# An eighth place for experts' weights in the second layer, another order of ring units in the first, and GpSimd's small loads behind the first two blocks

## The reference, cut to what matters

```
for l in range(2):
    mod = silu(cond) @ mod_w[l] + mod_b[l]            # 1024 x 6144 weights per layer
    sh1, sc1, g1, sh2, sc2, g2 = split(mod, 6)
    h = rms(x, norm_g[l, 0]) * (1 + sc1) + sh1
    if l == 0: out = ab_mixer(h, ab_in_w, ..., ab_out_w)   # HGRN2 recurrence | attention
    else:      out = hyena(h, hy_in_w, ..., hy_out_w)      # long convolution
    x = x + g1 * out
    h = rms(x, norm_g[l, 1]) * (1 + sc2) + sh2
    x = x + g2 * moe(h, router_w, router_b, w_gate[l], w_up[l], w_down[l])

def moe(h, ...):                                      # 16 experts, top 2 of one group of 4
    gates = routing weights, tokens x 16
    a = einsum('td,edf->etf', h, w_gate)              # w_gate, w_up: 16 x 1024 x 512
    b = einsum('td,edf->etf', h, w_up)
    hid = silu(a) * b * gates
    return einsum('etf,efd->td', hid, w_down)         # w_down: 16 x 512 x 1024
```

## Time and profile before

| | before |
|---|---|
| median of three runs | 874.86 us (872.3 to 875.55) |
| profiled execution | 872.13 us |
| its span | 869.9 us |
| TensorE busy | 820.4 us, 94% of the span |
| HBM read | 290.10 MB, 335 GB/s over the span |
| mean granted TensorE clock | 0.988 |

### The profile page before, as it was taken

How to read it: one execution, slowest core, us unless ns; L and a number is a source line. 1 busy time by engine, 2 the same in 40 slices (tenths; PEclk the granted TensorE clock), 3 DMA queues, 4 the chain that set the end, 5 groups by cost and what they waited for, 6 DMA issues and landing times.

```text
span 869.9 us, 13266 instructions
## 1 busy us (share of the span) xinstructions
PE 820.4 (94%) x5760; PEld 514.4 (59%) x5760; DVE 284.2 (33%) x587; ACT 176.4 (20%) x308; POOL 37.9 (4%) x67
## 2 busy tenths in 40 slices
PE   4999999799899999999999999999899999999997
PEld 3867778687643555345536888788643555345434
DVE  2155533614631211112114844662531212121113
ACT  4056013411511110111013212300411101110111
POOL 5000000030300000000000000000210000000000
PEclk8999999999999999999999999999899999999999
DMA  9999866652999999999999869255599999999981
GB/s 307 387 312 369 303 225 239 245 193 97 406 418 405 422 429 429 428 429 428 429 407 386 296 245 333 100 192 196 209 387 394 419 430 429 428 429 429 428 364 50
DMA packets 60004, 292.53 MB, mean 336 GB/s; under 512 B 2993, under 2 KB 5158, under 8 KB 47604
## 3 DMA queue, kind: packets, MB, share of 16 engines
q1 hardware_dynamic: 57940, 289.69, 83.5%
q10 hardware_dynamic: 1248, 1.08, 0.5%
q0 software_dynamic: 768, 1.04, 0.5%
HBM read 290.10 MB, written 1.70 MB: 335 GB/s over the span
## 4 chain that ended last, share of the span: by engine, by line
PE 70%; DMA 20%; DVE 7%; issue 1%; ACT 1%; SPq 1%; DVEq 0%
PE ps L1887 20%; DMA ring<-in_moe_w_up 17%; PE ps L1910 7%; PE ps L2018 6%; PE ps L1477 4%; PE ps L1541 4%; PE ps L1873 4%; PE ps L1663 3%; PE ps L1749 3%; PE ps L1535 3%; PE ps L1516 3%; PE ps L1923 2%; DMA ring<-in_mod_w 2%; PE ps L2014 1%; DVE hs L1117 1%
## 5 line engine op out<-in xcount | busy, mean ns | idle before, releaser
L1887 PE MATMUL ps<-ring,arena 128*64 128x512 f32 x896 | 224.7, 593 | 12.4 <-DMA ring<-in_moe_w_up 10.7
L1887 PEld LDWEIGHTS ps<-ring,arena 128*64 128x64 f32 x896 | 75.8, 137 | 118.6 <-issue 116.6
L1910 PE MATMUL ps<-ring,arena 128*64 128x512 f32 x512 | 113.4, 595 | 1.1 <-ACT arena L798 1.1
L1910 PEld LDWEIGHTS ps<-ring,arena 128*64 128x64 f32 x512 | 36.2, 137 | 66.4 <-issue 63.2
L1268 DVE SCALAR_TENSOR_TENSOR arena<-ps,arena 128x256 f32<-128x256 f32 x32 | 20.0, 668 | 163.0 <-PE ps L1887 163.0
L2018 PE MATMUL ps<-hs,ring 128*128 128x256 f32 x320 | 70.3, 380 | 0.0
L2018 PEld LDWEIGHTS ps<-hs,ring 128*128 128x128 f32 x320 | 60.5, 190 | 9.3 <-issue 1.4
L1873 PE MATMUL ps<-arena 128*128 (+1 forms) x512 | 60.0, 275 | 0.0
L1873 PEld LDWEIGHTS ps<-arena 128*128 128x128 f32 x512 | 58.4, 192 | 0.4 <-issue 0.4
L1887 PE MATMUL ps<-hs,arena 128*64 128x512 f32 x128 | 56.3, 593 | 0.0
L1477 PE MATMUL ps<-ring,csil 128*32 128x128 f32 x1536 | 51.2, 290 | 4.4 <-DVE arena L909 4.1
(11 more groups left out here) (310 smaller groups left out, 837.5 us busy)
## 6 DMA issues: line engine op xcount, KB each, us to landing
ring<-in_moe_w_up SPq DMA_DIRECT2D x32, 2048.0 KB, 17.2
ring<-in_moe_w_down SPq DMA_DIRECT2D x32, 2048.0 KB, 13.3
ring<-in_mod_w SPq DMA_DIRECT2D x24, 2048.0 KB, 12.7
ring<-in_moe_w_gate SPq DMA_DIRECT2D x24, 2048.0 KB, 13.9
hs<-in_moe_w_gate SPq DMA_DIRECT2D x8, 2048.0 KB, 17.4
ring<-in_hy_in_w SPq DMA_DIRECT2D x6, 2048.0 KB, 12.7
ring<-in_ab_in_w SPq DMA_DIRECT2D x4, 2048.0 KB, 13.1
ring<-in_ab_in_w SPq DMA_DIRECT2D x5, 1024.0 KB, 18.7
```

Of the source, the lines that this page charges most:

```text
L1887: ins = mm(bank(4 + w)[e * 64:e * 64 + 64, :], xg[:, k, e * 64:e * 64 + 64], weights[:, k, :], start=(k == 0), stop=(k == KD - 1))
L1910: ins = mm(bank(6 + half)[e * 64:e * 64 + 64, :], hidT[:, f, e * 64:e * 64 + 64], down_unit(n + 4 + e)[:, f, half * 512:half * 512 + 512], ...
```

## The change

Three edits. First, in layer 1 a second extra place, `late_spare`, for the gate of the pair's second expert in even pairs (odd pairs have it in its ring place), with an own order of the loads. Second, modulation blocks 14 and 15 come ahead of the two units of the output projection in the ring's order, so they have places 1 and 2, and the output projection places 3 and 4; the four small tables are now loaded behind both units of the output projection. Third, GpSimd waits for the arrival of modulation blocks 0 and 2 before its eleven small loads.

```
+UNITS += MODS[14:16]
 OUT0_AT = len(UNITS)
-UNITS += [("about", 0), ("about", 1)] + MODS[14:16]
-
+UNITS += [("about", 0), ("about", 1)]
...
+        late_spare = arena[:, 11776:11776 + UNIT].rearrange("p (k c) -> p k c", k=KD)
...
-                    if n == OUT0_AT + 3:
+                    if n == OUT0_AT + 2:
...
-                def load_gate(i, dst):
-                    sp.wait_ge(ring_free[n % RING], i + (n // RING - 1))
-                    arrived(sp, n, i - 1)
-                    load(i, 0, dst)
+                def load_gate(i, j, dst):
+                    m = n + j
+                    sp.wait_ge(ring_free[m % RING], i + (m // RING - 1))
+                    arrived(sp, m, i - 1)
+                    load(i, j, dst)
+                if l == 0:
...
+                else:
+                    sp.wait_ge(q["t_y"], 2)
+                    arrived(sp, n + 1 - RING)
+                    load(0, 1, late_spare)
+                    load_in_place(0, (0,))
+                    load_gate(1, 1, unit(n + 1))
+                    load_in_place(0, (2, 3, 4, 5))
+                    sp.wait_ge(q["t_htm"], 2 * l + 2)
+                    load_gate(1, 0, spare)
+                    for i in range(1, NPAIR):
+                        if i > 4:
+                            load_in_place(i, (2, 3, 4, 5))
+                        if i == 4:
+                            load_in_place(i, (2, 3))
+                        if i + 1 < NPAIR:
+                            load_gate(i + 1, 0, unit(n) if i % 2 else spare)
+                            load_gate(i + 1, 1, late_spare if i % 2 else unit(n + 1))
+                        if i == 4:
+                            load_in_place(i, (4, 5))
+                        if i < 4:
+                            load_in_place(i, (2, 3, 4, 5))
...
+            for m in (0, 2):
+                arrived(pool, MOD_AT[m])
...
-                                weights = spare if odd and w == 0 and e == 0 else unit(n + 2 * w + e)
+                                weights = unit(n + 2 * w + e)
+                                if w == 0 and e == 0 and odd:
+                                    weights = spare
+                                elif w == 0 and e == 1 and l == 1 and not odd:
+                                    weights = late_spare
```

More of the change, by code:

```diff
@@ L481, in load_in_place @@
                         load(i, j, down_unit(m) if j >= 4 else unit(m))
-                def load_gate(i, dst):
-                    sp.wait_ge(ring_free[n % RING], i + (n // RING - 1))
-                    arrived(sp, n, i - 1)
-                    load(i, 0, dst)
[L489 to L496, removed]
+                def load_gate(i, j, dst):
[4 more added lines that the diff above has]
+                if l == 0:
+                    load_in_place(0, range(6))
+                    sp.wait_ge(q["t_htm"], 2 * l + 2)
+                    load_gate(1, 0, spare)
+                    for i in range(1, NPAIR):
+                        load_in_place(i, (1,))
+                        if i + 1 < NPAIR:
[8 more added lines that the diff above has]
+                    load_in_place(0, (2, 3, 4, 5))
+                    sp.wait_ge(q["t_htm"], 2 * l + 2)
+                    load_gate(1, 0, spare)
+                    for i in range(1, NPAIR):
+                        if i > 4:
+                            load_in_place(i, (2, 3, 4, 5))
+                        if i == 4:
+                            load_in_place(i, (2, 3))
+                        if i + 1 < NPAIR:
+                            load_gate(i + 1, 0, unit(n) if i % 2 else spare)
+                            load_gate(i + 1, 1, late_spare if i % 2 else unit(n + 1))
+                        if i == 4:
+                            load_in_place(i, (4, 5))
+                        if i < 4:
+                            load_in_place(i, (2, 3, 4, 5))
                 n += 6 * NPAIR
```

## The result

The changed kernel took 866.18 us (median of six runs, 865.59 to 869.36), the kernel before 873.24 us (six runs, 871.88 to 875.55). The ratio is 0.9943 with a 95% interval of 0.9921 to 0.9965: faster, by 0.35 to 0.79%. (The two medians by themselves lie 7.1 us apart, which is 0.9919. The text goes by the ratio.) The profiled execution took 866.14 us, with a span of 863.9 us where it was 869.9.

The account below looks back on a forecast made before the run. Bound by DMA in the experts, with TensorE close behind: 29.4 against 27.49 us a pair. Layer 1 -4.1, layer 0 +0.3, start -0.3 us: 874.86 - 4.1 = 870.8 us; range 868.7 to 872.2, 8 in 10 within 867.3 to 873.6.

Parts of the forecast that it names:

- dry issue: Expert loads: a unit issued into a nearly empty queue lands 8.4 to 9.9 us later, taken as 9.3.
- pair 3's wait: Layer 1: TensorE's wait of 0.77 us at pair 3's ups stays.
- The downs of pair 4: Layer 1: landing at 765.9, wanted at 766.25, close but in time.
- The detail of 0.2 us: Layer 1, pair 2's first gate: the other gate now stands behind it on SP, costing 0 to 0.5 us.
- a loss of 0.3 us: Layer 0's other ring order: two-unit lead lost at a dry queue; bounds 1.0 us gain, 0.8 loss.
- The small loads: Start: GpSimd's eleven loads cost 1.2 us of DMA; moving them removes block 2's 0.28 us wait, gain 0.3.
- B: Rival: nothing lost at dry issues, layer 0 gains 1.0; 7.1 us gained in all, 867.8 us; chance 0.20.
- C: Rival: layer 1's lead does not arrive, pair 4's downs hold TensorE; 1.6 us gain, 873.3 us; chance 0.17.
- D: Rival: queue runs dry at every pair's downs from pair 5 on; slower, 878.1 us; chance 0.06.
- E: Rival: shifted times bring or spare a half-clock stretch of TensorE; 1.7 us either way, 869.1 or 872.5; chance 0.09.
- The estimate of 6.8 us: Expert loads: the skill's rule, 2.0 us fixed plus bytes at 436 GB/s, gives 2 MiB issue to landing.

Follow-up runs that it names:

- The place without the turn: Kernel before plus layer 1's eighth place; all pairs keep the order next gates, then ups, then downs: 0.9991.
- the turn without the place: Kernel before, seven places; in layer 1 from pair 4 on a pair's ups go ahead of gate 0 of the next pair: 0.9967.
- place and turn alone: Changed kernel without its two other edits: layer 1's eighth place, and ups ahead of next gates from pair 4; 0.9919 to the kernel before.
- the three with the turn in layer 0: Changed kernel with ups ahead of the next pair's gate 0 from pair 4 in layer 0 too, first run: 0.9895, 861.64 us; two further runs follow.
- ring order as before: Changed kernel with that order in layer 0 too, but blocks 14 and 15 put back behind the output projection: 0.9885, 861.89 us.
- again: Changed kernel with that order in layer 0 too, run once more on the same chip as the one with ring order put back: 0.9902, 862.15 us.

## Why the prediction was right, and where it was off

**The mechanism.** The rows of before gave two paces, 27.49 us for TensorE and 29.4 for DMA, and the statement that the place brings nothing until the order turns at pair 4. The place without the turn and the turn without the place show both halves of it. The waits went at pairs 4 to 6 and a small one came at pair 7's ups, as forecast. The reading of the page was off by one or two slices, and no term uses it: counted from one, the rate stands at 428 to 430 GB/s in slices 15 to 20 and 33 to 38.

**Layer 1, mis-sized.** Forecast 4.1 us, measured 5.62 in the pair of profiles. Over all profiles layer 1 takes 224.7 to 225.5 us with neither place nor turn (five, mean 225.2) and 219.4 to 220.7 with both (five, mean 220.0): 5.1 us, at the upper bound of 5.1 that went with 8.4 us for each dry issue. The term that was mis-sized is the 9.3 us for a dry issue. The ups of pair 4 took 9.6 us from issue to landing, the downs of pair 5 8.3. The first of these downs landed at 780.7 and not at 782.6: 1.0 us is the shorter landing, 0.9 the earlier issue (772.45 instead of 773.3), and so pair 7's ups waited 0.39 us, not 1.4. The issue was earlier because pair 3's wait, forecast to stay, was gone: the downs of pair 1, a dry issue too, landed after 8.7 us instead of 9.7. That is scatter: with place and turn this wait is 0, 0.99, 0.67, 0 and 0.51 us in five profiles (the order is changed kernel, place and turn alone, then the three with the turn in layer 0: first, ring order as before, again), and layer 1 takes 219.5, 220.7, 220.2, 219.4 and 220.3 us, longer where this wait is. With the wait at 0.99 the gain was 4.4 us, close to the 4.1 that were forecast with it in place. The downs of pair 4, close by the working, landed at 765.2 and did not wait.

Two smaller terms were off. The detail of 0.2 us shows as pair 1's ups landing 0.8 us later, counted from the first gate product (32.4 instead of 31.6), for which nobody waited. And the last down products were to start 10.6 us after pair 7's ups, with their weights there at 846.2; they started 11.0 us after them, since they waited 0.73 us for a unit that landed at 845.5. The last two units took 11.0 us to land (834.55 to 845.53) and not 9.8. The kernel before had the same (837.46 to 848.53), where TensorE came too late to notice.

**Layer 0, not contradicted.** Forecast a loss of 0.3 us, measured 0.55 in the two profiles and nothing that can be told in the run times (1.0006). That 0.3 and 0.55 are close is luck: in the seven profiles that have layer 0's order of before, its experts take 224.0 to 227.4 us (mean 225.4), and the two with the new ring order alone 224.8 and 224.9. What the forecast had right is that no wait shrinks. Counted from the first gate product, gate 1 of pair 1 landed after 15.5 us where it was 17.0 before, since its issue took 8.3 us and not 9.9. But the first down of pair 1 took 9.5 us where it was 8.4, and landed after 38.0 us where it was 37.0. So in this pair the lead lived one step longer than the working had it, and was gone at the next.

**The start, right in size as far as the profiles tell, with a term too small.** The small loads delay block 2 by 3.2 us in the mean of the profiles and not by 1.2. The working took the rate of one window of 5 us (295 against 387 GB/s), while the loads were in flight from 7.6 to about 20 us. What was forecast as the gain, 0.28 us, is the wait of that one profile; others without the edit waited from nothing up to 1.22 us for block 2 and 0.85 us for the next unit. In the changed kernel's 0.79 us, 0.43 are the earlier arrival of `x_sample` (7.82 instead of 8.25), which lies anywhere from 7.6 to 9.1 in these profiles. So what the edit brings in a single run lies between nothing and 2 us, the mean of 0.3 us at the projection's start agrees with the forecast, and the run times do not settle it.

**The sum.** -4.1 us was forecast, and the ratio of 0.9943 is -5.0 on 873.24 (-3.1 to -6.9 by its interval). In the pair of profiles it was -6.0, and there the missing part lies mainly in layer 1, 1.5 us, and at the start, 0.5 us. The absolute 866.18 us lies 1.1 below the stated range; the kernel before, too, ran 1.6 us below the 874.86 that the forecast started from once it had six runs. Of the rivals, B (nothing lost at dry issues, and layer 0 gains) has a number for layer 1, 5.8 us, that the 5.62 of this pair comes close to, but not for its reason: pair 4's ups still landed 7.1 us after the unit ahead of them and pair 5's downs 5.7 us, where 4.89 would be no loss. Its second half, a gain in layer 0, did not come. C and D did not come: pair 6's ups landed at 805.2, after pair 5's downs had been used at 799.97. E did not show in this pair of profiles: the same half-clock stretches appear in both, from about 15 to 22 us and at about 141, 158 and 616 us. In other profiles stretches are missing, with a price that can be read off (last section).

The estimate of 6.8 us for a 2 MiB load, which the prediction worked out from the Trainium skill's fit for loads that GpSimd issues ("DMA: Bandwidth & Descriptors", section "Anatomy of one DMA — SWDGE (gpsimd) path"), was not seen. These loads are SyncE's: the lowest of any 2 MiB load in these profiles is 7.6 us, and 8.0 among the expert loads.

## What to carry to other kernels

When TensorE and DMA are within a few per cent, follow the landings unit by unit, and ask for each wait which unit it is for and what was issued ahead of it that is wanted later. Here a deeper buffer for something else did not move it (0.9991). A change in the order of issue did (0.9967 in one layer, 0.9948 in both), and the buffer paid only in so far as it let that order turn further. Fetching ahead is right while the queue would run empty, and costs once DMA is the bound. Where that turn is best made was not tried: every kernel here that turns does so at pair 4.

## What the runs showed of the hardware that was not expected

A unit of experts that is issued with at most 4 us of work ahead of it lands 8.0 to 10.5 us after its issue in these profiles, and what is left does not settle where in that range: with 3.1 us left it took 8.4 us in layer 0 and 9.7 in layer 1 of the same execution. In a steady queue units land 4.89 us apart. And eleven small loads of 0.27 MB in all delay a 2 MiB load beside them by 3.2 us, where their bytes at 387 GB/s would be 0.7 us.

The granted clock of TensorE differs between executions of nearly the same program. Here are the windows 141.8 to 145.2 and 158.9 to 162.2 us (columns as in the earlier trace rows) of the kernel before, at about half clock, 1.2 GHz, in both:

```profile
141.80:145.20 3.40, 3.40 (x54) 2.85 (x48) 1.02 (x5) 0.00 (x0) 1.90 (x4) 0.51 1.04 393
158.90:162.20 3.30, 3.30 (x23) 3.08 (x24) 1.29 (x2) 0.01 (x1) 0.00 (x0) 0.50 1.02 398
```

And here are the same windows of the kernel with the ring order alone, at full clock, 2.4 GHz, in both:

```profile
141.80:145.20 3.40, 3.40 (x76) 2.74 (x64) 1.31 (x6) 0.00 (x0) 1.91 (x4) 1.00 1.05 395
158.90:162.20 3.30, 2.44 (x17) 1.61 (x15) 2.81 (x4) 1.67 (x3) 0.00 (x0) 1.00 1.07 385
```

In the first window it ran 76 products where the kernel before ran 54. With a lowered clock in both stretches (0.50 to 0.60 over the windows) layer 0's experts start at 238.3 to 239.6 us (five profiles), with one in the second alone (0.67 to 0.90, as it does not fill the window) at 236.4 to 238.0 (four), with neither at 235.4 to 237.1 (four). The groups differ in other things too: GpSimd's edit is in one, one and three of them, and three of the four with the second alone also lack the half-clock stretch between about 14 and 25 us that the others have. But without GpSimd's edit in either, the ring order alone starts its experts at 236.20 us and the kernel before at 239.12. So up to 3 us of the scatter of a single run goes with stretches that come and go in work that no edit touched, and the 0.3 us that GpSimd's edit brings in the mean is lost in it.
